# An mLSTM step on one core: the normalizer's sum moved from GpSimd to VectorE, and one fill's added tile and low part moved behind the next step's state products

## The reference, cut to what matters

```python
S = einsum('bhtd,bhsd->bhts', qc, kc) * exp(D - mt[..., None])
num = einsum('bhts,bhsd->bhtd', S, vc) + w_inter[..., None] * einsum('bhvk,bhtk->bhtv', C, qc)
den = sum(S, axis=-1) + w_inter * einsum('bhk,bhtk->bht', n, qc)
h = num / maximum(abs(den), exp(-mt))[..., None]
C_new = decay[..., None, None] * C + einsum('bhs,bhsv,bhsk->bhvk', ws, vc, kc)
n_new = decay[..., None] * n + einsum('bhs,bhsk->bhk', ws, kc)
```

## Time and profile before

| | |
|---|---|
| median of 3 runs (lowest to highest) | 1363.09 us (1362.47 to 1364.18) |
| the profiled execution | 1361.84 us |
| its span, first to last instruction | 1360.1 us |
| mean granted TensorE clock | 0.996 |
| busy PE / DVE / ACT / POOL | 1326.0 / 915.9 / 613.9 / 78.3 us |

### The profile page before, as it was taken

How to read it: one execution, slowest core, us unless ns; L and a number is a source line. 1 busy time by engine, 2 the same in 40 slices (tenths; PEclk the granted TensorE clock), 3 DMA queues, 4 the chain that set the end, 5 groups by cost and what they waited for, 6 DMA issues and landing times.

```text
span 1360.1 us, 24760 instructions
## 1 busy us (share of the span) xinstructions
PE 1326.0 (97%) x10087; PEld 1287.9 (95%) x10087; DVE 915.9 (67%) x1438; ACT 613.9 (45%) x1038; POOL 78.3 (6%) x65
## 2 busy tenths in 40 slices
PE   6999999999999999999999999999999999999997
PEld 6999898899999999999999988989999999999997
DVE  6666786789567376476666767876975845846733
ACT  5324334468427247156242333344771642732732
POOL 2000001100000000000510000020000000000032
PEclk8999999999999999999999999999999999999999
DMA  7321220032223223132252222202223222222311
GB/s 213 94 68 63 63 64 32 31 97 77 92 69 118 93 63 123 62 93 93 77 123 68 63 68 58 63 32 71 71 93 94 79 97 73 93 93 62 123 62 70
DMA packets 115625, 110.18 MB, mean 81 GB/s; under 512 B 18830, under 2 KB 109398, under 8 KB 115414
## 3 DMA queue, kind: packets, MB, share of 16 engines
q1 hardware_dynamic: 110320, 105.32, 25.4%
q10 hardware_dynamic: 5222, 3.71, 1.0%
HBM read 105.21 MB, written 3.81 MB: 80 GB/s over the span
## 4 chain that ended last, share of the span: by engine, by line
PE 82%; DVE 7%; issue 5%; ACT 3%; POOL 1%; DMA 0%; SPq 0%; DVEq 0%; ACTq 0%; POOLq 0%
PE psum L1569 54%; PE psum L1866 7%; PE psum L1868 7%; PE psum L1867 7%; DVE z L1187 1%; PE psum L1703 1%; PE psum L1823 1%; POOL nq L508 1%; DVE w_lo L982 1%; DVE x L1079 1%; PE psum L1734 1%; PE psum L1730 1%; PE psum L1721 0%; PE psum L1645 0%; PE psum L1723 0%
## 5 line engine op out<-in xcount | busy, mean ns | idle before, releaser
L1569 PE MATMUL psum<-hid_h,w_hi 128*128 128x288 f32 x1264 | 274.0, 298 | 0.8 <-DVE x L1079 0.8
L1569 PE MATMUL psum<-hid_h,w_lo 128*128 128x288 f32 x1264 | 270.5, 296 | 0.0
L1569 PE MATMUL psum<-hid_l,w_hi 128*128 128x288 f32 x1264 | 270.5, 296 | 0.0
L1569 PEld LDWEIGHTS psum<-hid_h,w_hi 128*128 128x128 f32 x1264 | 203.2, 189 | 1.8 <-DVE x L1079 1.2
L1569 PEld LDWEIGHTS psum<-hid_h,w_lo 128*128 128x128 f32 x1264 | 203.5, 189 | 0.0
L1569 PEld LDWEIGHTS psum<-hid_l,w_hi 128*128 128x128 f32 x1264 | 203.5, 189 | 0.0
L1569 PE MATMUL psum<-xh,w_hi 128*128 128x288 f32 x800 | 178.2, 304 | 8.1 <-DVE w_lo L982 4.5
L1482 DVE TENSOR_TENSOR tmp<-psum,rms 128x576 f32<-128x576 f32 x64 | 48.5, 758 | 193.4 <-PE psum L1569 193.3
L1569 PE MATMUL psum<-xh,w_lo 128*128 128x288 f32 x800 | 171.7, 296 | 0.0
L1569 PE MATMUL psum<-xl,w_hi 128*128 128x288 f32 x800 | 171.4, 296 | 0.0
L768 ACT ACTIVATE w_hi<-stage 128x1024 fp32r<-128x1024 f32 x64 | 67.8, 1059 | 220.7 <-PE psum L1569 219.8
(11 more groups left out here) (326 smaller groups left out, 2595.5 us busy)
## 6 DMA issues: line engine op xcount, KB each, us to landing
stage<-in_w_up SPq DMA_DIRECT2D x32, 1024.0 KB, 5.5
stage<-in_w_down SPq DMA_DIRECT2D x32, 1024.0 KB, 5.0
stage<-in_w_in SPq DMA_DIRECT2D x18, 1024.0 KB, 5.2
stage<-in_w_in SPq DMA_DIRECT2D x16, 256.0 KB, 4.5
stage<-in_w_out SPq DMA_DIRECT2D x8, 512.0 KB, 6.2
stage<-in_w_out SPq DMA_DIRECT2D x4, 1024.0 KB, 5.1
z<-in_x_prompt SPq DMA_DIRECT2D x4, 512.0 KB, 6.2
out<-z SPq DMA_DIRECT2D x4, 512.0 KB, 3.7
```

Of the source, the lines that this page charges most:

```text
L1569: ins = M(acc[t % 2][:, a, :], lhs(w), mov[:, k, a * HALF:(a + 1) * HALF], start=first and n == 0, stop=last and n == 2)
```

## The change

The normalizer's sum `nq + sw` is taken out of GpSimd's program and put into VectorE's, as `den_sum(p)`, behind the state update of head 3 and ahead of those of heads 0 to 2. The third fill of step p is taken from the end of step p in VectorE's program and put into step p + 1, behind `new_state(p + 1)` and ahead of `low_part(p)`; the last step's stays at the end. No instruction of TensorE, ScalarE or SyncE moves.

```diff
@@ gpsimd
                     nc.gpsimd.tensor_tensor(wsv[0:r, :, 0:MD], vtok[0:r], w.to_broadcast([r, MH, MD]), ALU.mult).then_inc(s_wv, 1)
-                    if p:
-
-                        pool.wait_ge(s_nq, (NP - 1) * l + p)
-                        nc.gpsimd.tensor_tensor(nq[0:r, :, 0:r], nq[0:r, :, 0:r], sw[0:r, :, 0:r], ALU.add).then_inc(s_dn, 1)
                 squares(2 * l + 2)
@@ vector
+                def den_sum(p):
+
+                    r = rows(p)
+                    dve.wait_ge(s_nq, (NP - 1) * l + p)
+                    dve.wait_ge(s_sw, NP * l + p + 1)
+                    V.tensor_tensor(nq[0:r, :, 0:r], nq[0:r, :, 0:r], sw[0:r, :, 0:r], ALU.add).then_inc(s_dn, 1)
+
                 def new_state(p):
...
                         if h == MH - 1:
                             ins.then_inc(s_nn, 1)
+                            if p:
+                                den_sum(p)
                     ins.then_inc(s_st, 1)
...
                     new_state(p)
                     if p:
+                        fill("m", p - 1, 2)
                         low_part(p - 1)
                     fill("m", p, 0)
...
                     V.tensor_tensor(hm, z[:, 4:8, pair_cols(p)], rs, ALU.mult).then_inc(s_hm, 1)
-                    fill("m", p, 2)
+                fill("m", NP - 1, 2)
                 low_part(NP - 1)
```

## The result

The median of 5 runs is 1356.63 us (1355.79 to 1356.71); the kernel before, beside it, 1362.48. The two medians are 5.85 us apart; the ratio on record, which is not that of the medians, is 0.9947, with a 95% interval of 0.9935 to 0.9959: faster by 0.53%. The profiled execution took 1355.79, its span 1354.0.

What follows compares the result with a forecast made beforehand. TensorE, busy nearly throughout, bounds the kernel; only its waits can be given back. Per layer 0.48 + 1.30 + 0.67 - 0.06 + 0.20 - 0.08 = 2.51, two layers 5.0 us: 1363.09 - 5.0 = 1358.1; range 1356.5 to 1360.8.

Steps and rivals of the forecast that it cites:

- Both waits: TensorE's state products L1814 waiting for `qw` (1.30 us, step 2) and normalizer's product L1823 for GpSimd's sum (0.66, 0.67, 0.20).
- Step 1's sum: On VectorE it takes 0.69 us, so L1823 starts at 225.81 instead of 226.29: 0.48 gained, ends 0.22 and 0.66.
- The state's updates: Step 1: updates of heads 0 to 2 queue behind the sum; transposes L1770 wait until 226.59, covered by 0.04 us.
- GpSimd's next `wsv`: Step 2: could hold L1287, but comes at 241.09, a third of a microsecond after L1287 starts; costed at nothing.
- The other queues: SyncE's next weight loads and the tile's PSUM bank come free 2.5 us later, at no cost; POOL issues no load.
- Rival 1: Low part L1287 stays long, or the maximum is late otherwise: 0.52 us less per layer, 1359.1; chance 0.2.
- rival 4: Sum works, but L1814 is still held, so step 2 gives only 0.67 us: 2.7 in all, 1360.4; chance 0.05.
- rivals 2 and 3: Gain given back later, as at a load, 1363.1, chance 0.12; slower, VectorE bound through step 2's maximum, 1366, chance 0.03.
- What is late next: Step 2: moved pair delays VectorE's low part L1287 and the maximum, so TensorE's scores L1756 wait: 0.06 us lost.
- the same term in step 3: The maximum releases scores L1756 at 254.99, where TensorE stands at 254.91: 0.08 us lost, 0.34 with the long L1287.
- signs of being wrong: Idle time of 0.3 us or more at L1756 (rival 1), at L1770 for the state, at L1814 still, or unshortened span.
- The 5.3 us: Two layers' gain if, by the skill page's port rule, L1756 would not wait at all in steps 2 and 3.

Runs made afterwards that it cites:

- the move alone: Third fill's tile and low part moved, sum still on GpSimd, against the kernel before: ratio 0.9976, stage 65.44 us.
- the first four experiments: Ratios to the kernel before: only the sum moved 0.9981; only the fills moved 0.9976; changed kernel with only step 1's pair moved 0.9952, with two more fills moved 0.9941.
- the two that were run side by side: The changed kernel again, 1356.10 us, 0.9946 of the kernel before; and it with two more fills moved, again, 1353.23 us, 0.9930.

## Why the prediction was right in kind and too small

**Right.** Both waits went at the places named, for the reasons named. Step 1's sum gave 0.48 as worked out (the sum 0.68, not 0.69). The state's updates came late enough to hold the first transpose's load, and this cost nothing: from the normalizer's product to the transposes it is 226.37 - 225.41 = 0.96 in the matmuls, as before (227.25 - 226.29). The low part went back to 0.68 with GpSimd's sum gone, and the run with GpSimd reading beside it stretched it again, and with the move alone it was short where GpSimd's sum was out of its way, so the cause is shown. GpSimd's next `wsv` did stay behind the low part, but by 0.11 us and not by a third: the prediction looked at L504, and the copy L503 goes ahead of it (240.44, against 240.33 for L1292). The other queues cost nothing. Rival 1 (the long low part) and rival 4 (the state products still held) did not come about, and there was no sign of rivals 2 and 3: from the first stage's end to the second's start it is 592.93 us in both profiles (868.35 - 275.42 and 865.13 - 272.20).

**The step that failed** is "What is late next", with the same term in step 3; and the sum put at nothing what a held product loses beyond its wait. The scores' load came late by 0.13 in step 2 (0.37 of idle time where 0.24 stood before) and by 0.12 in step 3, where 0.06 and 0.08 were worked out. The forecast took such lateness off the gain in full. It cost nothing: the load that follows (L1757, now L1763) used to come 0.43 behind L1756 (244.51 to 244.94), and comes 0.29 behind in the changed kernel (241.67 to 241.96). The two loads, before and after:

```profile
244.94 0.19 PEld L1757 LDWEIGHTS psum<-rconst,acl 128*128 128x128 f32 x1 [0.24 <-issue]
```

```profile
241.96 0.19 PEld L1763 LDWEIGHTS psum<-rconst,acl 128*128 128x128 f32 x1
```

TensorE's sequence of short loads had slack behind the late one; what the 0.24 before such a load consists of is not shown. The run with GpSimd beside VectorE gives the same from the other side: 0.2 of 0.98 free. Two of the prediction's own signs of being wrong misled for this reason. The 0.37 at the scores is over the 0.3 that was to mean rival 1, a sign that left out the 0.24 that stood there before; and the transposes did wait for the state. Neither cost anything. The 5.3 us that the prediction gives for scores that wait for nothing comes closer to what the stages gave, but by luck: it needs a low part of 0.56, and L1292 took 0.68.

**The term that was left out** is what a held product loses beyond its idle time. The matmuls of step 2, before:

```profile
239.00 1.16 PE L1814 MATMUL psum<-qw,cst 128*128 128x128 f32 x8 [1.06 <-DVE qw L1257]
239.92 0.64 PE L1817 MATMUL psum<-bcr,rconst 128*128 128x128 f32 x4
241.08 1.13 PE L1823 MATMUL psum<-nq,io 128*128 128x512 f32 x2 [0.53 <-POOL nq L508]
242.05 0.60 PE L1770 MATMUL psum<-io,z 128*128 128x128 f32 x4
```

and after:

```profile
236.89 1.05 PE L1820 MATMUL psum<-qw,cst 128*128 128x128 f32 x8
237.70 0.64 PE L1823 MATMUL psum<-bcr,rconst 128*128 128x128 f32 x4
238.18 1.07 PE L1829 MATMUL psum<-nq,io 128*128 128x512 f32 x2
239.09 0.60 PE L1776 MATMUL psum<-io,z 128*128 128x128 f32 x4
```

From the first to the second row it is 0.92 when held and 0.81 when not; from the third to the fourth 0.97 and 0.91. That is 0.11 and 0.06 for starting up again. It goes with being held and not with the kernel: in step 3 of the kernel before, where nothing held the state products, it is 0.81 too (252.57 to 253.38). What TensorE does in that time is not shown. Against it stands what a load does when it is not held. In the changed kernel:

```profile
236.49 0.32 PEld L1575 LDWEIGHTS psum<-hid_h,w_lo 128*128 128x128 f32 x2
236.76 0.99 PEld L1820 LDWEIGHTS psum<-qw,cst 128*128 128x128 f32 x8
```

The second starts 0.05 before the first has ended (236.81) and 0.13 before its own matmul (236.89); the held load started together with its matmul. So 1.30 of idle time at the load was worth 1.30 + 0.05 - 0.13 = 1.22 at the matmul, where the table has 1.23. Over step 2 these come to 0.79 + 1.23 = 2.02 in place of 1.97, and the 0.06 for starting up behind the normalizer's product is what stands in the table at step 3's state products (0.06) and at step 4's (0.05). The layer gave 2.82 and not 2.51, two layers 5.6 and not 5.0: of the 0.31 per layer, 0.14 is the two losses that did not occur, and 0.17 is this term with a few hundredths of rounding.

**The rest.** 5.6 us is the lower end of what the ratio's interval allows (5.6 to 8.9); the middle, 7.2, is not explained by the stages, so 1.6 of the 2.2 us between the forecast and 1355.9 stay open. The other kernels speak for scatter. Taken from 1363.09, the ratios of the first four experiments say 2.6, 3.3, 6.5 and 8.0 us, where their two stages give 2.5, 3.6, 5.6 and 7.9; those of the two that were run side by side say 7.4 and 9.5, where the stages give 5.7 and 7.9. So the excess seems to go with the set of executions, and not with the change. In the last set the kernel before had a median of 1364.12, against 1362.48 and 1362.61 in the other two, which can make up the excess there; for the first comparison, whose two medians lie 5.85 apart, it is not explained. In two profiles of the changed kernel the start of the first stage lay 1.0 us apart, and a low clock at the end costs 1.1 to 1.5, so executions differ by such amounts outside the changed work; whether the runs compared here fell unevenly in this way was not shown, and stays open. At its lower end the forecast's range left 0.9 for scatter, less than that.

## What to carry to other kernels

Price an operation on a second engine at the place where it stands in that engine's order: the sum behind one state update gained 2 x 1.25 us alone; behind four, with the fills moved, the stage was 0.88 longer than with the sum left on GpSimd. Work that only has to be done some time (an added tile, a low part) belongs behind the instruction that another engine waits for, and the same rule found two more such places here. Here the products that waited lost 0.07 less at the matmul than their loads stood idle (the state products and the projection), and 0.06 to 0.11 more for starting again, while a lateness of 0.1 to 0.2 ahead of a run of short loads may be free: terms of hundredths should be carried as a range around zero, not as a loss.

## What the runs showed of the hardware

**One GpSimd addition was held for 1.7 us.** GpSimd's 128x512 addition took 1.27 alone and 3.00 beside a 128x1024 low part and a 128x512 one on VectorE, both with two inputs in SBUF. In the changed kernel GpSimd's copy of four columns shows it too, 0.63 in step 2 where it was 0.19 in step 1:

```profile
227.72 0.19 POOL L503 COPY wsv<-gT 128x4 f32<-128x4 f32 x1 [12.12 <-ACT vtok L698]
...
240.44 0.63 POOL L503 COPY wsv<-gT 128x4 f32<-128x4 f32 x1 [11.53 <-ACT vtok L698]
```

It costs nothing there, since `wsv` is written by 242.07 and needed from 247.12.

**The clock at the two ends differs from execution to execution, and its record can miss a fall.** TensorE is idle from about 10.5 to 15 us, while it waits for the first weights, and in nine of the ten profiles the granted clock then falls to 0.50, the lower of its two levels, for some 7 us. In the changed kernel's second profile it reads 1.00 in that whole stretch, but the matmuls say otherwise: in the microsecond from 17 us six of them ran there, as many as at 0.50 in the first profile, and two take 0.68 us, where the same two take 0.42 or 0.43 from 20 us on. From the second profile, and from the first:

```profile
17.00:18.00 1.00, 1.00 (x6) 1.00 (x5) 1.00 (x2) 0.00 (x0) 1.00 (x1) 1.00 1.07 305
```

```profile
17.00:18.00 1.00, 1.00 (x6) 0.98 (x6) 1.00 (x1) 0.00 (x0) 1.00 (x1) 0.50 1.05 308
```

So a granted clock of 1.00 is to be checked against the matmuls under it. Near the end TensorE has another gap, of 0.4 us, and in two of the eight experiment profiles the clock fell under the work behind it (0.64 and 0.60 in that window): the last 32 matmuls took 5.3 us there, and 3.7 in the changed kernel's first profile, after the same gap. So a fraction of a per cent in this kernel is best read from the stage that was changed, which repeats within 0.03 us, and not from one span.
